# Retention scores and four channel means of a two-block kernel, taken from split operands in the rounded format instead of from full float32

## The reference

```python
def rmsnorm(x, g):
    y = xf * lax.rsqrt(jnp.mean(xf * xf, axis=-1, keepdims=True) + EPS)
def retention(q, k, v):                      # 12 heads, keys of 64, values of 128
    qf = rotary(q.reshape(B, S, H, dk), pos)
    kf = rotary(k.reshape(B, S, H, dk), pos) * (dk ** -0.5)
    ...
    inner = jnp.einsum('bhnd,bhmd->bhnm', qc, kc) * d_inner[None]
    o = jnp.einsum('bhnm,bhme->bhne', inner, vc)
    ...
def layer_norm(x, g, b):
    mu = jnp.mean(xf, axis=-1, keepdims=True)
```

## Time and profile before

| | us |
|---|---|
| median of 3 runs | 1815.93 (1815.48 to 1816.66) |
| the profiled execution's own time | 1815.78 |
| its span, first to last instruction | 1814.1 |
| TensorE busy in the span | 1806.9 |
| VectorE, GpSimd, ScalarE busy | 942.2, 789.3, 773.1 |

### The profile page before, as it was taken

The page is one execution under the profiler, slowest core; times in us unless marked ns, Lnnn a source line. Parts: engine busy times, 40 slices in busy tenths (PEclk is TensorE's granted clock), DMA queues, the critical chain, the costliest instruction groups (busy, mean ns, idle before and its releaser), DMA issues.

```text
span 1814.1 us, 23727 instructions
## 1 busy us (share of the span) xinstructions
PE 1806.9 (100%) x8577; PEld 1506.6 (83%) x8577; DVE 942.2 (52%) x1607; ACT 773.1 (43%) x1240; POOL 789.3 (44%) x380
## 2 busy tenths in 40 slices
PE   9999999999999999999999999999999999999998
PEld 7888888888888888888888888888888888888887
DVE  6246556554111666654259989956333564544202
ACT  5344444443333666643343233257323474444213
POOL 3444444444444333444444543353444454444442
PEclk9999999999999999999999999999999999999999
DMA  5333333333333323332333433322333333333332
GB/s 176 100 93 82 93 82 88 111 87 105 92 93 109 100 81 93 105 93 88 98 93 93 113 88 90 75 82 70 95 102 93 93 94 93 94 103 104 96 101 93
DMA packets 285751, 173.99 MB, mean 96 GB/s; under 512 B 14800, under 2 KB 271208, under 8 KB 285664
## 3 DMA queue, kind: packets, MB, share of 16 engines
q1 hardware_dynamic: 275264, 164.70, 31.7%
q0 software_dynamic: 2496, 8.07, 1.6%
q10 hardware_dynamic: 7904, 0.06, 0.2%
HBM read 170.62 MB, written 2.19 MB: 95 GB/s over the span
## 4 chain that ended last, share of the span: by engine, by line
PE 99%; DVE 0%; ACT 0%; issue 0%; DVEq 0%; ACTq 0%
PE proj L2208 23%; PE proj L2210 23%; PE proj L2209 23%; PE A L2541 1%; PE A L2543 1%; PE A L2542 1%; PE A L2904 1%; PE A L2905 1%; PE A L2906 1%; PE A L2366 1%; PE A L2463 1%; PE PV L2463 1%; PE proj L2543 1%; PE proj L2542 1%; PE proj L2541 1%; PE A L2456 1%
## 5 line engine op out<-in xcount | busy, mean ns | idle before, releaser
L611 POOL TENSOR_TENSOR wlo<-wraw,whi 128x1024 fp32r<-128x1024 f32 (+1 forms) x304 | 723.8, 2385 | 918.4 <-ACT whi L766 914.2
L766 ACT ACTIVATE whi<-wraw 128x1024 fp32r<-128x1024 f32 (+1 forms) x303 | 317.5, 1049 | 613.4 <-DMA wraw<-w_in 168.4
L2208 PE MATMUL proj<-Hh,whi 128*128 128x512 f32 x1424 | 562.5, 395 | 0.0
L2210 PE MATMUL proj<-Hh,wlo 128*128 128x512 f32 x1424 | 555.1, 390 | 0.0
L2209 PE MATMUL proj<-Hl,whi 128*128 128x512 f32 x1424 | 554.7, 390 | 0.0
L2210 PEld LDWEIGHTS proj<-Hh,wlo 128*128 128x128 f32 x1424 | 267.3, 188 | 56.3
L2208 PEld LDWEIGHTS proj<-Hh,whi 128*128 128x128 f32 x1424 | 267.5, 188 | 55.1 <-issue 0.7
L2209 PEld LDWEIGHTS proj<-Hl,whi 128*128 128x128 f32 x1424 | 267.6, 188 | 54.0 <-issue 0.7
L1835 DVE SCALAR_TENSOR_TENSOR A<-cin,dwT,A 128x512 f32<-128x512 f32 x232 | 175.1, 755 | 6.8
L2208 PE MATMUL proj<-Oh,whi 128*128 128x512 f32 x256 | 99.8, 390 | 0.0
L2209 PE MATMUL proj<-Ol,whi 128*128 128x512 f32 x256 | 99.6, 389 | 0.0
(11 more groups left out here) (561 smaller groups left out, 3045.2 us busy)
## 6 DMA issues: line engine op xcount, KB each, us to landing
wraw<-w_in SPq DMA_DIRECT2D x68, 512.0 KB, 3.9
wraw<-fox_w_in SPq DMA_DIRECT2D x56, 512.0 KB, 3.8
wraw<-ret_w_in SPq DMA_DIRECT2D x44, 512.0 KB, 3.8
wraw<-w_up SPq DMA_DIRECT2D x44, 512.0 KB, 3.9
wraw<-w_out SPq DMA_DIRECT2D x40, 512.0 KB, 4.1
wraw<-w_down SPq DMA_DIRECT2D x22, 512.0 KB, 3.5
wraw<-w_mem_kv SPq DMA_DIRECT2D x16, 512.0 KB, 3.9
wraw<-conv_pw_w SPq DMA_DIRECT2D x8, 512.0 KB, 4.1
```

The costliest lines, as they stand in the source:

```text
L611: pool.tensor_tensor(wlo[s][:, 0:r, :], wraw[s][:, 0:r, :], whi[s][:, 0:r, :].bitcast(F32), ALU.subtract).then_inc(w_lo, 1)
L766: f(whi[s][:, 0:r, :], wraw[s][:, 0:r, :], ACT.Copy).then_inc(w_hi, 1)
L2208: mm(dst, whi[s][:, c, :], xh, start=(first and c == 0), stop=False)
L2210: ins = mm(dst, wlo[s][:, c, :], xh, start=False, stop=(last and c == chunks - 1))
```

## The change

Scores: the rotation's last addition is made twice. Once it is written in the rounded format (the high part; for the keys this stands in the place where the plain sum stood), once in float32 as before, and then the difference is the low part. The scores are three passes over the eight products: key high by query high, key high by query low, key low by query high. They add up in the banks. Each pass has the wait inside it, and from the second pass on (0, 2) also waits for the (1, 2) of the pass before, because both write to PV.

Means: VectorE (for the layer norm's mean ScalarE and VectorE) splits the sum into high and low, and two products in the rounded format with `mean_r` take the place of one in float32. The low part is written over the sum. The two sums of the second layer now stand inside the second block of `glu`, before its fifth chunk.

```diff
@@ rope
+                high, low = roped_high[b], roped_low[b]
+                if b == 0:
+                    own.mark(tt(high, dst[:], swapped, ALU.add))
+                else:
+                    tt(high, dst[:], swapped, ALU.add).then_inc(r_low_made, 1)
                 tt(dst[:], dst[:], swapped, ALU.add).then_inc(r_roped, 1)
+                if b == 0:
+                    own.settle()
+                else:
+                    dve.wait_ge(r_low_made, k_high_count(i))
+                dve.wait_ge(r_roped, i * 2 + (b + 1))
+                tt(low, dst[:], high.bitcast(F32), ALU.subtract).then_inc(r_low_made, 1)
@@ after the first layer (the second: the same for acc and acc2)
+            def split_sum(high, low, total):
+
+                own.mark(dve.tensor_copy(high[:], total[:]))
+                own.settle()
+                tt(low[:], total[:], high[:].bitcast(F32), ALU.subtract).then_inc(r_low_made, 1)
...
+            dve.wait_ge(acc_done, KC)
+            split_sum(r_high[0], acc_low, acc)
@@ ret_scores
-                pe.wait_ge(r_roped, i * 2 + 2)
+                pe.wait_ge(r_low_made, k_high_count(i))
...
-                for e, j in ((0, 0), (1, 0), (0, 2), (1, 1), (0, 1), (1, 3), (0, 3), (1, 2)):
-                    rows = slice(DK * e, DK * e + DK)
-                    if (e, j) == (1, 2):
-                        pe.wait_ge(r_half, i + 1)
-                    ins = mm(ret_place(e, j), k[rows, j * P:(j + 1) * P], q[rows, j * P:S], start=True, stop=True)
-                    if (e, j) == (0, 2):
-                        ins.then_inc(r_half, 1)
+                for n, (x, y) in enumerate(((roped_high[1], roped_high[0]), (roped_high[1], roped_low[0]), (roped_low[1], roped_high[0]))):
+                    if n == 2:
+                        pe.wait_ge(r_low_made, k_low_count(i))
+                    for e, j in ((0, 0), (1, 0), (0, 2), (1, 1), (0, 1), (1, 3), (0, 3), (1, 2)):
+                        rows = slice(DK * e, DK * e + DK)
+                        if (e, j) == (1, 2):
+                            pe.wait_ge(r_half, 5 * i + 2 * n + 1)
+                        if (e, j) == (0, 2) and n:
+                            pe.wait_ge(r_half, 5 * i + 2 * n)
...
+                        if (e, j) == (0, 2) or (e, j) == (1, 2) and n < 2:
+                            ins.then_inc(r_half, 1)
@@ means on TensorE
-                pe.wait_ge(acc_done, k)
-                mm(bank[:], mean_d[:], source[:], start=True, stop=True).then_inc(stats, 1)
+            def mean_of(bank, high, low):
+
+                mm(bank[:], mean_r[:], high[:], start=True, stop=False)
+                return mm(bank[:], mean_r[:], low[:], start=False, stop=True)
...
-            statistics(2 * KC)
-            pe.wait_ge(sq2_summed, 1)
-            statistics(2 * KC, A[0], acc2)
-            products("glu", 0, 1, 1, H)
+            def final_sums(c):
+                if c == 4:
+                    statistics(squared_low(HEADS - 1) + 1, VT, r_high[0], acc_low)
+                    statistics(squared_low(HEADS - 1) + 2, A[0], r_high[1], acc2_low)
+
+            products("glu", 0, 1, 1, H, each=final_sums)
@@ the layer norm's mean: ScalarE, VectorE, TensorE
+                    act.wait_ge(c_summed, KC - 1)
+                    f(c_high[:], c_sum[:], ACT.Copy).then_inc(c_summed, 1)
+                    dve.wait_ge(c_summed, KC)
+                    tt(c_low[:], c_sum[:], c_high[:].bitcast(F32), ALU.subtract).then_inc(c_summed, 1)
-                        pe.wait_ge(c_summed, KC - 1)
-                        mm(A[3][:], mean_d[:], c_sum[:], start=True, stop=True).then_inc(l_mean, 1)
+                        pe.wait_ge(c_summed, KC + 1)
+                        mean_of(A[3], c_high, c_low).then_inc(l_mean, 1)
```

More of the change, by code:

```diff
@@ L142, in build @@
         mean_d = sb("mean_d", [P, P])
+        mean_r = sb("mean_r", [P, P], F32R)
         vec = sb("vec", [P, V_COLS])
@@ L146, in build @@
         rms = sb("rms", [P, S])
+        with ExitStack() as summed:
+            acc_low = sb("acc_low", [P, S], F32R, summed)
         acc = sb("acc", [P, S])
@@ L195, in build @@
             probsT = sb("probsT", [P, 1280], F32, one)
+            with ExitStack() as summed:
+                acc2_low = sb("acc2_low", [P, S], F32R, summed)
             z0, gate0 = sb("z0", [P, S], F32, one), sb("gate0", [P, S], F32, one)
@@ L217, in build @@
             decay = [sb(f"decay{e}", [P, S], F32, one) for e in range(2)]
-            mean_r = sb("mean_r", [P, P], F32R, one)
         f_x, f_a, f_b, f_one = probs[0:HEADS, 0:S], probs[0:HEADS, S:2 * S], probsT[0:HEADS, 0:S], probsT[0:HEADS, S:2 * S]
@@ L224, in build @@
         decayed_low = (probs_high[:], turned_low[:])
+        roped_high, roped_low = (Oh[:, HEADS + 3, :], Ol[:, HEADS + 3, :]), (qm_high[:], qm_low[:])
         maskf, acc2 = sq2[:, 0:P], z[0]
@@ L252, in build @@
                 dstat = sb("dstat", [P, 64], F32, dil)
+                with ExitStack() as summed:
+                    c_low = sb("c_low", [P, S], F32R, summed)
                 c_sum = sb("c_sum", [P, S], F32, dil)
+                c_high = sb("c_high", [P, S], F32R, dil)
                 c_sq_sum = sb("c_sq_sum", [P, S], F32, dil)
@@ L340, in build @@
         sq_ready, sq2_ready, acc_done = sem("sq_ready"), sem("sq2_ready"), sem("acc_done")
-        stats, rms_ready, sq2_scaled, sq2_summed = sem("stats"), sem("rms_ready"), sem("sq2_scaled"), sem("sq2_summed")
+        stats, rms_ready, sq2_scaled = sem("stats"), sem("rms_ready"), sem("sq2_scaled")
         f_step, f_act, c_ready = sem("f_step"), sem("f_act"), sem("c_ready")
@@ L499, in squared, with q_low_count, k_high_count, k_low_count @@
             return weighed(r) + 2
+        def q_low_count(i):
+            return 7 * i + 2
+        def k_high_count(i):
+            return 7 * i + 3
+        def k_low_count(i):
+            return 7 * i + 4
+        def weighed_low(r):
+            return 7 * (r // 2) + r % 2 + 5
+        def squared_low(r):
+            return 7 * (r // 2) + r % 2 + 7
         def split_values(group, j):
@@ L1195, in d_stage @@
                     layer_norm(b)
+                if last and b == 2:
+                    act.wait_ge(c_summed, KC - 1)
+                    f(c_high[:], c_sum[:], ACT.Copy).then_inc(c_summed, 1)
                 if h:
@@ L1781, in _ @@
                 softmax_turn("mem0", i, i + HEADS, "mem" if i else "fox", i + (HEADS - 1))
+            def split_sum(high, low, total):
+                own.mark(dve.tensor_copy(high[:], total[:]))
+                own.settle()
+                tt(low[:], total[:], high[:].bitcast(F32), ALU.subtract).then_inc(r_low_made, 1)
+            dve.tensor_copy(mean_r[:], mean_d[:]).then_inc(v_rooted[1], 1)
             wo_turn("wo0", 0, HEADS + MEM_HEADS)
@@ L1792, in _ @@
             own.settle()
-            dve.tensor_copy(mean_r[:], mean_d[:]).then_inc(v_rooted[1], 1)
             dve.wait_ge(v_spread[1], 1)
@@ L1814, in _ @@
             own.settle()
-            dve.sem_inc(sq2_summed, 1)
+            dve.wait_ge(acc_done, 2 * KC)
+            split_sum(r_high[0], acc_low, acc)
+            split_sum(r_high[1], acc2_low, acc2)
             dve.wait_ge(rms_ready, 3)
@@ L2447, in ret_scores @@
             def ret_scores(i):
-                pe.wait_ge(r_roped, i * 2 + 2)
+                pe.wait_ge(r_low_made, k_high_count(i))
                 since(pe, r_decayed, i * 2)
                 since(pe, r_out, i * 2)
-                for e, j in ((0, 0), (1, 0), (0, 2), (1, 1), (0, 1), (1, 3), (0, 3), (1, 2)):
-                    rows = slice(DK * e, DK * e + DK)
-                    if (e, j) == (1, 2):
-                        pe.wait_ge(r_half, i + 1)
-                    ins = mm(ret_place(e, j), k[rows, j * P:(j + 1) * P], q[rows, j * P:S], start=True, stop=True)
-                    if (e, j) == (0, 2):
-                        ins.then_inc(r_half, 1)
+                for n, (x, y) in enumerate(((roped_high[1], roped_high[0]), (roped_high[1], roped_low[0]), (roped_low[1], roped_high[0]))):
[7 more added lines that the diff above has]
+                            pe.wait_ge(r_half, 5 * i + 2 * n)
+                        first = n == 0 and (e, j) in ((0, 0), (1, 0), (0, 2), (1, 1), (0, 1))
+                        ins = mm(ret_place(e, j), x[rows, j * P:(j + 1) * P], y[rows, j * P:S], start=first, stop=(n == 2 and (e, j) in ((0, 0), (1, 0), (0, 3), (1, 3), (1, 2))))
+                        if (e, j) == (0, 2) or (e, j) == (1, 2) and n < 2:
+                            ins.then_inc(r_half, 1)
                 ins.then_inc(r_scores, 1)
@@ L2474, in ret_values_low @@
             def ret_values_low(r, e):
-                pe.wait_ge(r_low_made, weighed(r))
+                pe.wait_ge(r_low_made, weighed_low(r))
                 for j in range(NT):
@@ L2481, in ret_mean @@
             def ret_mean(r, e):
-                pe.wait_ge(r_low_made, squared(r))
+                pe.wait_ge(r_low_made, squared_low(r))
```

(12 more changed lines are left out.)

## The result

The changed kernel took 1822.6 us (median of 6 runs, 1821.9 to 1824.3) beside 1816.1 for the kernel before: ratio 1.0037, 95% interval 1.0027 to 1.0048. The forecast was 1818.5 with a range to 1822.0; +2.6 us was expected and about +6.5 came. The profiled execution took 1823.18, 7.4 more than that of before.

The account below looks back on a forecast made before the run. TensorE, holding 99% of the chain of waits, was taken as the bound. Links +2.3, start stall +1.65, means -1.67 and late weights +0.32 made +2.6 us: 1818.5 us, range 1813.2 to 1822 (forecast's own 1816.5 to 1820.5).

Parts of the forecast that it names:

- The links: Scores: five waits a turn chained through bank PV, 0.44 us each; +0.38 a turn, +2.3 us in six turns.
- Its sign against itself: Scores on TensorE: the forecast is wrong if PV products follow each other at less than 0.4 us.
- The stall at the start: Before the scores: TensorE waits 0.33 us for VectorE's keys in turns two to six, not the first; +1.65 us.
- The means and the late weights: Rounded means save 1.67 us; GpSimd's low weights come 0.32 us late at the second `glu` turn's second block.
- The queries' low part costs nothing: Rotation: it lies in the 2.43 us for which VectorE waits for ScalarE's copy; uncovered it would add 0.7.
- The keys' low part: Rotation on VectorE: ends at 623.24, before the third score pass at 623.62, so 0.33 us in hand.
- the heads take turns: Rival, scores: the halves don't overlap in the rounded format; 3.6 us a turn, +1.36 each, 1824.4 us; chance 0.10.
- The forecast's other sign: Chain of waits: the forecast is wrong if VectorE or ScalarE turn up anywhere but the two places named.

Follow-up runs that it names:

- the two runs without the hold: Against the changed kernel: GpSimd's fourth split waits for the keys' low part, or the keys' plain sum is written into PSUM bank VT; each 1818.76 us.
- GpSimd later: Changed kernel, but GpSimd's fourth weight split of a retention turn waits until the keys' low part is made; 1818.76 us, ratio 1.0015.
- the run with one link: Changed kernel with GpSimd's fourth split waiting for the keys' low part and score products reordered so PV changes heads once a turn; 1817.68 us, ratio 1.0009.

## Why the prediction was wrong

- **The links**: right. Five of 0.44 and +0.38 a turn were forecast; 0.33 and four of 0.44, and +0.36 a turn, came in the two runs without the hold, which stand 2.9 us above before where the forecast had 2.6. Its sign against itself, PV products at less than 0.4, did turn up (the 0.33), but that is how records start: the first product's begins with its stream, the next one's with its load, 0.11 ahead of its stream.
- **The stall at the start**: right. 0.33 in five turns, none in the first; 0.38 in five (623.17 - 622.47 = 0.70 for 0.32), none in the first.
- **The means and the late weights**: right, -1.62 for -1.67 and +0.34 for +0.32.
- **The queries' low part costs nothing**: right in its result, but by luck: in turns two to six it was held too, took up to 1.72 us and not 0.69, and only the wide cover hid it (VectorE still waited 0.60 us or more for ScalarE's copy in every turn).
- **The keys' low part**: the step that failed. The forecast took it to be 0.69 us long, right behind the plain sum's end at 622.52, let it end at 623.24, "so 0.33 is in hand", and put the third pass's wait at nothing. It took 1.68 to 2.84 us, and the third pass waited for it in all six turns. By the blocks of the six turns, 20.87 us after and 16.33 with GpSimd later, that is 4.5 us on TensorE; by the medians 3.8 (1822.6 to 1818.76, twice, by two edits that have nothing in common but this hold), or 3.6 with each set against its own kernel before; the intervals allow any of these. The forecast plus 3.8 is 1822.3.

What should have been seen was in the trace of before. The forecast took a duration from the neighbours of the new instruction, and those had an operand in PSUM. VectorE's instruction with two operands in SBUF in the same turn (`ztanh` and `z`) has two durations there:

```profile
602.53 1.40 DVE L1702 SCALAR_TENSOR_TENSOR gate<-ztanh,z 128x512 f32<-128x512 f32 x1 [1.40 <-ACT ztanh L952]
606.86 0.68 DVE L1702 SCALAR_TENSOR_TENSOR gate<-ztanh,z 128x512 f32<-128x512 f32 x1
```

and GpSimd's row in that stretch of the kernel before, and its row at the second turn's scores, say which is which:

```profile
600.64 2.75 POOL L611 TENSOR_TENSOR wlo<-wraw,whi 128x1024 fp32r<-128x1024 f32 x1 [1.13 <-ACT whi L766]
```

```profile
621.41 2.36 POOL L611 TENSOR_TENSOR wlo<-wraw,whi 128x1024 fp32r<-128x1024 f32 x1 [3.00 <-ACT whi L766]
```

The first split ends at 603.39, 0.86 after the gate begins, and 0.86 + 0.55 is 1.41, for 1.40; all six turns have it (1.40 each). At 606.86 none runs. From the last row the price could have been worked out: the split ends at 623.77, so a low part that begins at about 622.55 has 1.22 of it ahead, takes 1.77 and ends at 624.32; the third pass, forecast for 623.62, would start at 624.37, 0.75 late, 4.5 us in six such turns. The forecast asked only whether there was cover for 0.69.

The Trainium skill, "SBUF — State Buffer", section "Who interferes with whom", has this rule: a VectorE instruction with two inputs in SBUF contends with a GpSimd instruction that reads SBUF. The Trainium skill's same page, section "SBUF: two separate sides", says that whichever of the two starts first gets the shared ports for its whole length and the other is fully blocked. The runs here agree on all three points: two inputs (1.68 to 2.84 us) against one (0.69, with a split beside it throughout), the wait to the split's end, and the order (0.69 for every low part that began ahead of the split; 2.94 for one, in the first turn of the run with one link, that began 0.01 us behind it).

One sign that the forecast named would have misled. It said that 3.6 us for the scores means that the heads take turns, which was the rival with +1.36 a turn; the turns came out at 3.3 to 3.7 and +1.33 to +1.54, nearly its price. But that rival's row is the second head's stream beginning at the end of the first's, and the first two products stand in one row of 0.50 us. The size of a loss doesn't identify it; the row that waits does. The forecast's other sign, VectorE in the chain in a place other than the two named, was the one that told.

## What to carry to other kernels

Before an instruction is priced by its neighbours' duration, see where its operands lie: here VectorE's with both in SBUF were priced by what GpSimd ran at that moment, and the same instruction with one operand in PSUM was not. Such an instruction that others wait for can be moved out of GpSimd's way by making GpSimd wait, where its own work has slack, or by leaving one operand in PSUM; here both won the same. And where work is split into more passes into one bank, order the passes so that the bank changes hands once, since each change costs a full result, wait and load (0.44 us here), which was worth 1.9 us of TensorE's time in six turns.

## What the runs showed of the hardware

- VectorE's 128x512 instruction with both operands in SBUF, begun while GpSimd's 128x1024 split runs, lasts to the split's end and 0.55 us on (0.69 alone), in 11 of 11 such low parts of the changed kernel. Begun before the split, it isn't lengthened (0.69 with 0.40 to 0.61 us of the split inside it, five such parts in four runs).
- The hold goes the other way too: a 128x1024 split that GpSimd begins inside VectorE's `turned_low` (two operands in SBUF) takes 2.74 to 2.76 us in the changed kernel, six of six, and 2.36 to 2.42 where it begins with nothing running on VectorE.
- Rounded products on the two halves of TensorE's rows start 3 to 4 ns apart and stream together (two of 512 columns in 0.50 us), as the float32 records did (6 to 7 ns).
